# Chunk 12's bank read before the operand sums, one constant pair fewer at the router, a modulation product behind x's transposes, and a first weight chunk in halves

## What is computed

```
mod = silu(c) @ w_mod + b_mod             # 12 blocks of 512 columns: shift, scale, gate, twice
h   = x * (1 + scale1) + shift1
a, b, c, gates = h @ w_in + b_in          # 18 chunks of 512 columns, and 16 gate columns
y   = sum over three branches of sigmoid(g_i) * (branch_i @ w_branch_i)
x   = layer_norm(ALPHA * x + gate1 * (y @ w_out))
h   = x * (1 + scale2) + shift2
x   = layer_norm(ALPHA * x + gate2 * moe(h))   # 4 expert groups, best group, best 2 of its 4 experts
```

## Time and profile before

| | |
|---|---|
| median of three runs | 1401.21 us |
| the profiled execution | 1402.76 us |
| its span, from the first to the last instruction | 1400.8 us |
| TensorE matmuls busy | 1334.4 us (95%) |
| VectorE busy | 559.9 us (40%) |
| ScalarE busy | 233.7 us (17%) |
| GpSimd busy | 139.0 us (10%) |
| mean granted TensorE clock | 0.985 of full |
| DMA packets' bytes | 375.33 MB, 268 GB/s over the span |

### The profile page before, as it was taken

How to read it: one execution, slowest core, us unless ns; L and a number is a source line. 1 busy time by engine, 2 the same in 40 slices (tenths; PEclk the granted TensorE clock), 3 DMA queues, 4 the chain that set the end, 5 groups by cost and what they waited for, 6 DMA issues and landing times. The chain is left out here.

```text
span 1400.8 us, 18175 instructions
## 1 busy us (share of the span) xinstructions
PE 1334.4 (95%) x7172; PEld 816.3 (58%) x7172; DVE 559.9 (40%) x1058; ACT 233.7 (17%) x518; POOL 139.0 (10%) x115
## 2 busy tenths in 40 slices
PE   5999999899999999999979999998999999999994
PEld 2675586478645555555538656855874555555552
DVE  1224455456334522322352345554643443322324
ACT  0021221233201101111110213121430110111110
POOL 0003431012200000000000043401230000000000
PEclk9899999999999999999999999999999999999998
DMA  9755554556644999999984625353544829999993
GB/s 381 256 225 192 219 188 167 231 196 256 242 164 196 367 392 396 412 411 413 413 363 147 240 98 212 128 182 113 217 176 157 322 83 394 407 412 393 412 412 133
DMA packets 46030, 375.33 MB, mean 268 GB/s; under 512 B 15114, under 2 KB 19338, under 8 KB 23180
## 3 DMA queue, kind: packets, MB, share of 16 engines
q1 hardware_dynamic: 37536, 371.14, 66.5%
q10 hardware_dynamic: 8428, 3.29, 0.9%
HBM read 370.07 MB, written 4.33 MB: 267 GB/s over the span
## 5 line engine op out<-in xcount | busy, mean ns | idle before, releaser
L1091 PE MATMUL psum<-ring,hT 128*128 128x512 f32 x512 | 236.1, 610 | 4.2 <-ACT hT L1304 2.2
L1211 PE MATMUL psum<-ring,tbuf 128*64 128x256 f32 x1920 | 215.9, 380 | 0.9 <-DMA ring<-in_stream 0.9
L1211 PEld LDWEIGHTS psum<-ring,tbuf 128*64 128x64 f32 x1920 | 136.1, 137 | 93.6 <-issue 20.0
L1091 PEld LDWEIGHTS psum<-ring,hT 128*128 128x128 f32 x512 | 96.3, 196 | 113.0 <-issue 106.8
L1087 PE MATMUL psum<-hT,ring 128*128 128x256 f32 x640 | 143.1, 380 | 0.0
L1087 PEld LDWEIGHTS psum<-hT,ring 128*128 128x128 f32 x640 | 119.9, 190 | 18.3 <-issue 3.1
L1250 PE MATMUL psum<-ring,tbuf 128*64 128x512 f32 x512 | 116.9, 599 | 1.9 <-ACT tbuf L1516 1.9
L2005 DVE TENSOR_SCALAR tbuf<-tbuf 128x256 f32<-128x256 f32 x32 | 9.4, 294 | 240.7 <-ACT tbuf L1506 240.7
L1115 PE MATMUL psum<-ring,tbuf 128*128 128x512 f32 x192 | 82.7, 592 | 0.0
L2144 POOL TENSOR_SCALAR ldata<-ldata 128x512 f32<-128x512 f32 x24 | 51.2, 2135 | 244.4 <-ACT ldata L1443 244.4
L1250 PEld LDWEIGHTS psum<-ring,tbuf 128*64 128x64 f32 x512 | 33.9, 136 | 70.0 <-issue 59.4
(11 more groups left out here) (304 smaller groups left out, 1426.6 us busy)
## 6 DMA issues: line engine op xcount, KB each, us to landing
ring<-in_stream SPq DMA_DIRECT2D x154, 2048.0 KB, 9.2
ch<-in_stream SPq DMA_DIRECT2D x8, 2048.0 KB, 14.0
bias_ring<-in_b_in SPq DMA_DIRECT2D x26, 256.0 KB, 9.0
ldata<-in_ldata SPq DMA_DIRECT2D x2, 2329.0 KB, 19.2
tbuf<-in_stream SPq DMA_DIRECT2D x2, 2048.0 KB, 14.7
hbuf<-in_ln SPq DMA_DIRECT2D x4, 1024.0 KB, 9.1
hbuf<-in_stream SPq DMA_DIRECT2D x1, 2048.0 KB, 8.4
hbuf<-row_mem SPq DMA_DIRECT2D x2, 1024.0 KB, 11.2
```

Source lines behind the costliest of these rows:

```text
L1091: mm = pe.matmul(bank(PJ + g), hT[:, k, g * P:(g + 1) * P], w[:, k, :], start=(k == 0), stop=(k == KT - 1))
L1211: mm = pe.matmul(psum[halves_of[hf], UP[j], 0:FE // 2], xgT[:, k, halves_of[i]], w_up[:, k, hf * (FE // 2):(hf + 1) * (FE // 2)], start=(k ...
```

## The change

- **Chunk 12.** `a_sums` moves behind the eviction of chunk 12's group 0 in quarter 49; `first_sums(13)` moves to the end of quarter 51, behind the eviction of group 1.
- **Router.** One `hold_clock` matmul fewer in each layer: 3 become 2, and 5 become 4.
- **Modulation.** Only the first of the two blocks stays behind the expert loop; the second runs behind the transposes of x's group 0, in the place of two constant matmuls. The signal to ScalarE moves with it.
- **First chunk.** Chunk 0 of layer 0 is loaded as two halves of 1024 KB: blocks k = 0 to 3, then early blocks 2 and 3, then blocks k = 4 to 7, then the bias. Part 0 waits for the first half alone.

```
+            def first_chunk(i):
+
+                j = (RING_BASE[0] + i) % RING
+                source = dram["stream"][stream_slot("in", 0, 0)]
+                sp.wait_ge(slot_used, BASE[0] + (i + 1))
+                sp.dma_start(ring[:, j, 0:SLOT // 2], source[:, 0:SLOT // 2]).then_inc(first_half_loaded, 16)
+                load_early(2)
+                load_early(3)
+                sp.dma_start(ring[:, j, SLOT // 2:SLOT], source[:, SLOT // 2:SLOT]).then_inc(slot_loaded[j], 16)
+
...
-                    load(l, i)
+                    if (kind, c, l) == ("in", 0, 0):
+                        first_chunk(i)
+                    else:
+                        load(l, i)
...
-                    if (kind, c, l) == ("in", 0, 0):
-                        load_early(2)
-                        load_early(3)
...
+            def layer_mod(j):
+
+                pe.wait_ge(layer_mods_loaded[j], 16)
+                return mod_products(ahead_slot[j].rearrange("p (k n) -> p k n", k=KT), LAYER_MODS[j], 1, j == 0, j == 1)
...
                         if g == 0:
-                            hold_clock(2)
+                            layer_mod(1).then_inc(layer_mods_filled, 1)
...
-                    w = slot(l, "in", l, c)
+                    if (l, c, part) == (0, 0, 0):
+                        pe.wait_ge(first_half_loaded, 16)
+                        w = ring[:, (RING_BASE[l] + AT[l]["in", l, c]) % RING, :].rearrange("p (k n) -> p k n", k=KT)
+                    else:
+                        w = slot(l, "in", l, c)
...
-                    hold_clock(3, bank(7))
+                    hold_clock(2, bank(7))
                 else:
-                    hold_clock(5, bank(7))
+                    hold_clock(4, bank(7))
...
                 if l + 1 < DEPTH:
-                    for j, m in enumerate(LAYER_MODS):
-                        pe.wait_ge(layer_mods_loaded[j], 16)
-                        mm = mod_products(ahead_slot[j].rearrange("p (k n) -> p k n", k=KT), m, 1, j == 0, j == 1)
-                    mm.then_inc(layer_mods_filled, 1)
+                    layer_mod(0)
...
-                    if q == A_SUMS_AT:
-                        a_sums()
-                        first_sums(FAST[0])
                     if c in FAST:
                         fast_part(c, q % 4)
...
+                    if q == A_SUMS_AT:
+                        a_sums()
+                    if q == 4 * FAST[0] - 1:
+                        first_sums(FAST[0])
```

More of the change, by code:

```diff
@@ L414, in build @@
         slot_loaded = [sem(f"slot_loaded{i}") for i in range(RING)]
+        first_half_loaded = sem("first_half_loaded")
         bias_loaded = [sem(f"bias_loaded{i}") for i in range(RING)]
```

## The result

The changed kernel takes 1387.53 us (median of 4 runs, 1386.01 to 1389.50), the kernel before 1400.71 beside it: a ratio of 0.9903, 95% interval 0.989 to 0.9915, that is 13.6 us less (11.9 to 15.4); the two medians are 13.2 apart. The profiled execution took 1389.5 us with a span of 1387.7, against 1402.76 and 1400.8 before.

The account below looks back on a forecast made before the run. The prediction took a chain of TensorE work to bound the kernel. Gains of 4.0 + 4.95 + 5.7 + 0.7 + 0.4 + 0.5 = 16.25 us off the median 1401.21 gave 1385.0 us, range 1380.5 to 1391.

Parts of the forecast that it names:

- What bounds: Whole run: a chain of TensorE work, so its pauses and low-clock stretches are paid in full unless DMA sets the next stage's pace.
- First chunk by halves: Start of layer 0: the last early modulation block no longer waits for its load; 4.0 us gained, bounds 2.0 to 5.9.
- From 31.66 I go by full-clock rows: Start: last early block begins at 31.66 us, fold and block run at full clock, part 1 starts at 37.7 instead of 41.75.
- Chunk 12's bank first: Chunk 12, both layers: earlier eviction shortens the pause ahead of L948 and keeps the clock; 4.95 and 5.7 us gained.
- The clock's 3.3 us: Chunk 12, each layer: L948 and the eight products behind it take 4.8 us at full clock instead of 8.1.
- Rival (a): Clock falls in the new 1.4 us pause ahead of L948, one or both layers: 1388.3 or 1391.6 us; chance 0.14.
- One pair less: Ahead of the ranking in the router: one constant matmul pair fewer gains 0.7 us in layer 0, 0.4 in layer 1.
- rival (d): Clock falls ahead of the ranking and stays low into the expert loop: 3.3 us per 8 us low, 1402 to 1406; chance 0.02.
- Second modulation: Change of layers: transposes come 1.8 us earlier, but the first product waits for weights until 722.3; 0.5 us gained.
- the forecast's band: Total time of the changed kernel: 1382 to 1387.5 us, given a chance of 0.66.
- rival (b): Start: halves don't bring the last early block forward, as the extra transfer costs queue time; 1387 to 1389 us; chance 0.07.
- TensorE's total of 0.9 us for the ring says that it can: Expert loops: small total wait for the weight ring means the router's gains in both layers pass through the loop.

## Why the prediction was right, and where its steps were not

**What bounds.** Right: where a pause of TensorE or a low stretch went, the lead grew by as much, and from chunk 1 to the eviction of chunk 11 it stays at 2.9 us through 200 us of work.

**First chunk by halves.** The mechanism was right: the wait for the last block is gone, and the fold and blocks behind it have the full clock. The size was off, 2.9 in the pair of traces and 1.8 to 5.0 by the times of the halves alone. The step that failed is "From 31.66 I go by full-clock rows": the 31.66 hangs on the clock of the first fold, and where that runs low (nine of 14 profiles) TensorE is later and the load no longer the one that is waited for. The prediction took one start for the start. In the pair of traces this is the smaller share of the 1.1 us: part 1 starts at 38.07 for 37.7. The rest is part 1 itself, which the prediction let keep its 8.8 us (start of part 1 to start of chunk 1) and which has 9.56 there; over the 13 profiles with the pause ahead of it, it is 8.5 to 9.6.

**Chunk 12's bank first.** Both terms a little low: 5.4 and 6.2 against 4.95 and 5.7. The pause is 0.96 us and not 1.4, since GpSimd's step took 2.26 us beside VectorE's sums and not the 2.71 of the earlier trace rows. That VectorE pays as well is visible: one of the four sums took 0.98 us instead of 0.69, and T2 1.51 instead of 1.22. The Trainium skill, GPSIMD Engine Reference, section Specifications, names this contention for the shared SBUF interface; the trace agrees, at 0.33 us on GpSimd's side here. The clock's 3.3 us came out as forecast in these two traces, but that is luck in part: over the profiles with the old pause it is 2.7 in the mean. The prediction read the chain rightly (bank, sigmoid, GpSimd, credit), but looked at one way to cut it: moving the credit, with the bank as late as before, does the same. Rival (a), that 1.4 us would be enough for the clock to fall, had something for it: 1.25 us were enough in the filled pause of layer 1, 0.96 never in eight cases.

**One pair less.** 0.85 and 0.6 at the rankings, against 0.7 and 0.4. What it is worth in the end is nothing that can be told (0.1 us, -1.1 to 1.4), and rival (d) showed itself at the price of 1.63 us where it was given 3.3 and more.

**Second modulation.** Right to a few tenths, with the weights' landing as the bound (0.93 us of wait).

**The sum.** 16.25 us against 13.6 in the times: 1387.53 us lies in the range, 2.5 above the 1385.0, at the edge between the forecast's band and that of rival (b), which the trace rules out since the last block came in time. The parts at chunk 12 and the router came out 1.3 us better than forecast, which hides some of the 1.1 us of the start and the 3.5 us of the loops. The step that failed is the sentence that all must get through the expert loops and "TensorE's total of 0.9 us for the ring says that it can". It measured one trace of a quantity that differs: the loops give back 0 to 2.7 us each. The half-loaded weights show that the ring's loads do this in layer 0, and two traces with equal issues show that the same loads at the same instants took 7.5 or 10.2 us. Of the profiles with full loads, four of the five with the halves lose over 1 us in loop 0 (2.5, 2.3, 2.0, 2.7) and one of the eight without them (1.6); but equally four of the five that reach the loop at 452.5 to 453.7 us do, and one of the eight that reach it later. The one with the later sigmoid has both the halves and the early start, and loses nothing. Whether the halves or the earlier start make the loss likelier, or it is chance in the transfers alone, stays open.

## What to carry to other kernels

Before moving late work forward, ask which semaphore the waiting engine wants, and what else stands ahead of that credit in its engine's queue: here a change of one condition on ScalarE was worth as much as the reordering of VectorE. A pause of TensorE has two prices, its own length and the clock behind it; price the second from several executions, since it was 3.3 or 1.7 us behind the same pause in different profiles, and 1.63 or nothing behind another. And keep a ledger of leads at fixed instructions over several profiles: one pair of traces mixed up to 2 us of chance at the start and up to 2.7 us in a loop with the effects of the edits.

## What the runs showed of the hardware

The time that a stretch runs at the low clock comes in steps. The same 16 matmul records, behind pauses of 3.06 us in layer 0 and 3.84 in layer 1, took 8.1 us (six times) or 6.5 (four times) and nothing between, with both lengths in either layer; 32 small ones behind a pause of 0.90 us took 3.81 or 5.44, and the eight records of a fold behind 0.96 to 0.99 us took 1.05 or 1.89. The length of the pause alone doesn't decide it: the clock fell behind 1.25 us (the earlier trace rows show it hold over 1.7 us) and in three of 14 profiles behind the 0.90 us that follow the small matmuls of layer 1's ranking. A 2048 KB load split in two left what stood behind it in the full queue 0.23 to 0.37 us later, in one profile. And a 2048 KB load of the expert loop, issued at the same instant of two executions, took 7.5 us in one and 10.2 in the other.
